# Where the empty rounds of a data-dependent block loop stand: after the full ones, or ahead of them

## The reference, cut to what matters

```python
h = silu(einsum('td,edf->tef', xf, w_gate)) * einsum('td,edf->tef', xf, w_up)
y = einsum('tef,te,efd->td', h, gate, w_down)
```

## Time and profile before

| | us |
|---|---|
| median of 3 runs (lowest, highest) | 1498.01 (1496.25, 1498.43) |
| the profiled execution's own time | 1493.46 |
| span of the profiled execution | 1491.6 |
| TensorE busy | 1439.3 (96%) |
| VectorE busy | 1015.0 (68%) |
| ScalarE busy | 770.8 (52%) |

### The profile page before, as it was taken

The page is one execution under the profiler, slowest core; times in us unless marked ns, Lnnn a source line. Parts: engine busy times, 40 slices in busy tenths (PEclk is TensorE's granted clock), DMA queues, the critical chain, the costliest instruction groups (busy, mean ns, idle before and its releaser), DMA issues.

```text
span 1491.6 us, 24267 instructions
## 1 busy us (share of the span) xinstructions
PE 1439.3 (96%) x9396; PEld 1291.7 (87%) x9396; DVE 1015.0 (68%) x1287; ACT 770.8 (52%) x912; POOL 190.4 (13%) x99
## 2 busy tenths in 40 slices
PE   8999999999999999999997999999999999999995
PEld 7999999999999999999996467888888888888772
DVE  4246746757777787523125668888888888888877
ACT  4245545444434433411110047777777777777774
POOL 0000000000000000234330001121121211222130
PEclk9999999999999999999998899999999999999998
DMA  7321231322213312633435699999999999999997
GB/s 262 123 89 57 86 114 61 96 90 86 88 57 115 116 58 73 205 111 146 145 96 205 207 394 375 384 401 391 392 375 384 384 382 398 387 390 401 348 294 232
DMA packets 74389, 335.36 MB, mean 225 GB/s; under 512 B 12086, under 2 KB 18790, under 8 KB 45514
## 3 DMA queue, kind: packets, MB, share of 16 engines
q1 hardware_dynamic: 68842, 315.54, 56.2%
q0 software_dynamic: 5472, 18.74, 5.0%
HBM read 313.56 MB, written 40.73 MB: 238 GB/s over the span
## 4 chain that ended last, share of the span: by engine, by line
PE 85%; DVE 7%; DMA 3%; ACT 2%; issue 2%; POOL 0%; ACTq 0%; SPq 0%; DVEq 0%; POOLq 0%
PE BANK L1811 13%; PE BANK L1812 13%; PE BANK L1813 13%; PE BANK L2170 7%; PE BANK L2172 7%; PE BANK L2171 7%; PE BANK L2222 4%; PE BANK L2220 4%; PE BANK L2221 4%; PE BANK L2154 2%; DMA RAWB<-in_w_up 2%; PE BANK L2183 2%; PE BANK L1953 1%; PE BANK L1829 1%; PE BANK L2050 1%
## 5 line engine op out<-in xcount | busy, mean ns | idle before, releaser
L1811 PE MATMUL BANK<-XH,HI 128*128 128x260 f32 x1746 | 503.0, 288 | 1.4 <-DVE RT L1487 1.0
L1683 DVE TENSOR_TENSOR LOB<-RAWB,HIB 128x2048 fp32r<-128x2048 f32 x196 | 448.6, 2291 | 74.0 <-ACT HIB L1050 73.1
L1812 PE MATMUL BANK<-XL,HI 128*128 128x260 f32 x1746 | 495.3, 284 | 0.0
L1813 PE MATMUL BANK<-XH,LO 128*128 128x260 f32 x1746 | 494.3, 283 | 0.0
L1050 ACT ACTIVATE HIB<-RAWB 128x2048 fp32r<-128x2048 f32 x196 | 376.4, 1921 | 86.0 <-PE BANK L2172 66.1
L1811 PEld LDWEIGHTS BANK<-XH,HI 128*128 128x128 f32 x1746 | 331.2, 190 | 2.7 <-issue 1.7
L1812 PEld LDWEIGHTS BANK<-XL,HI 128*128 128x128 f32 x1746 | 331.1, 190 | 0.7
L1813 PEld LDWEIGHTS BANK<-XH,LO 128*128 128x128 f32 x1746 | 330.9, 190 | 0.0
L2170 PE MATMUL BANK<-HIB,XGH 128*128 128x512 f32 x512 | 201.8, 394 | 5.5 <-issue 3.0
L2172 PE MATMUL BANK<-LOB,XGH 128*128 128x512 f32 x512 | 200.0, 391 | 0.0
L2171 PE MATMUL BANK<-HIB,XGL 128*128 128x512 f32 x512 | 199.8, 390 | 0.0
(11 more groups left out here) (388 smaller groups left out, 1674.5 us busy)
## 6 DMA issues: line engine op xcount, KB each, us to landing
RAWB<-in_w_down SPq DMA_DIRECT2D x68, 1024.0 KB, 9.5
RAWB<-in_w_gate SPq DMA_DIRECT2D x67, 1024.0 KB, 9.4
RAWB<-in_w_up SPq DMA_DIRECT2D x67, 1024.0 KB, 8.9
RAW<-in_w_in SPq DMA_DIRECT2D x39, 1024.0 KB, 4.9
RAW<-in_w_out SPq DMA_DIRECT2D x16, 1024.0 KB, 5.0
Y<-in_xT SPq DMA_DIRECT2D x8, 520.0 KB, 9.1
RT<-in_xT SPq DMA_DIRECT2D x16, 260.0 KB, 5.2
x_rows<-R SPq DMA_DIRECT2D x5, 832.0 KB
```

The costliest lines, as they stand in the source:

```text
L1683: dve.tensor_tensor(LOB[:, s, :], RAWB[:, r, :], HIB[:, s, :].bitcast(F32), ALU.subtract).then_inc(b_lo[s], 1)
L1811: pe.matmul(bank, hw[:, c, :], h, start=(c == 0), stop=False)
L1812: pe.matmul(bank, hw[:, c, :], l, start=False, stop=False)
L1813: ins = pe.matmul(bank, lw[:, c, :], h, start=False, stop=(c == KC - 1))
```

## The change: what it does

The loops keep their number of rounds, but the loop's own counter (now k) no longer names the block. `empty` is MAXB - last, that is 8 here (MAXB + 1 - (nb - 1), 9 here, on SyncE, whose rounds start at 2). A round has a body if `empty < k`. So rounds 1 to 8 (2 to 9 on SyncE) are empty, and the full ones follow. The number of the block stands in a register of its own, set ahead of the loop and raised by one at the end of each body. The body is the same otherwise; it is entered with j = 1, 2, and so on as before. The diff for TensorE and for SyncE (VectorE, ScalarE and GpSimd as TensorE):

```diff
-            with pe.Fori(1, MAXB) as j:
-                with pe.If(j < last):
+            empty = pe.snap(MAXB - last)
+            block_no = pe.alloc_register("block_pe")
+            pe.reg_mov(block_no, 1)
+            with pe.Fori(1, MAXB) as k:
+                with pe.If(empty < k):
+                    j = pe.snap(block_no, min_val=1, max_val=MAXB - 1)
                     gate_up(j, 0)
                     for n in range(4):
                         tokens(n, j + 1)
                         down(n, 8 + n, j)
                     turn_h(j, 4 * j + 7)
+                    pe.reg_add(block_no, block_no, 1)
             gate_up(last, 0)
```

```diff
-            with sp.Fori(2, MAXB) as j:
-                with sp.If(j < nb - 1):
+            empty = sp.snap(MAXB + 1 - (nb - 1))
+            block_no = sp.alloc_register("block_sp")
+            sp.reg_mov(block_no, 2)
+            with sp.Fori(2, MAXB) as k:
+                with sp.If(empty < k):
+                    j = sp.snap(block_no, min_val=2, max_val=MAXB - 1)
                     gate_up(j, 0)
                     down(j, 8)
+                    sp.reg_add(block_no, block_no, 1)
             gate_up(nb - 1, 0)
```

More of the change, by code:

```diff
@@ L780, in _ @@
             gather(1, p_rows, YO)
-            with pool.Fori(1, MAXB) as j:
-                with pool.If(j < last):
+            empty = pool.snap(MAXB - last)
+            block_no = pool.alloc_register("block_pool")
+            pool.reg_mov(block_no, 1)
+            with pool.Fori(1, MAXB) as k:
+                with pool.If(empty < k):
+                    j = pool.snap(block_no, min_val=1, max_val=MAXB - 1)
                     pool.wait_ge(b_tx, 4 * j + 4)
@@ L790, in _ @@
                     scatter(j)
+                    pool.reg_add(block_no, block_no, 1)
             pool.wait_ge(b_yw, 16 * last)
@@ L1094, in _ @@
                 bhi(i, 0, 1)
-            with act.Fori(1, MAXB) as j:
-                with act.If(j < last):
+            empty = act.snap(MAXB - last)
+            block_no = act.alloc_register("block_act")
+            act.reg_mov(block_no, 1)
+            with act.Fori(1, MAXB) as k:
+                with act.If(empty < k):
+                    j = act.snap(block_no, min_val=1, max_val=MAXB - 1)
                     for i in range(7, 10):
@@ L1119, in _ @@
                         bhi(i, 0, j + 1)
+                    act.reg_add(block_no, block_no, 1)
             for i in range(7, 10):
@@ L1711, in _ @@
                 token_lo(g, 1)
-            with dve.Fori(1, MAXB) as j:
-                with dve.If(j < last):
+            empty = dve.snap(MAXB - last)
+            block_no = dve.alloc_register("block_dve")
+            dve.reg_mov(block_no, 1)
+            with dve.Fori(1, MAXB) as k:
+                with dve.If(empty < k):
+                    j = dve.snap(block_no, min_val=1, max_val=MAXB - 1)
                     h_lo(j - 1)
@@ L1725, in _ @@
                     blo(1, 0, j + 1)
+                    dve.reg_add(block_no, block_no, 1)
             h_lo(last - 1)
```

## The result

The changed kernel takes 1506.32 us in the median of 20 runs, the kernel before 1497.52 us in 20 runs on the same chip. The ratio is 1.0058, with a 95% interval of 1.0047 to 1.0068: the change costs 8.7 us (7.0 to 10.2). The forecast was +3.8 us, 1501.8 us with a range to 1505.8. The direction was right; the size was less than half of what came, and the time lies outside the range.

The account below looks back on a forecast made before the run. TensorE, busy 96% of the span, was taken as the bound, so only its stalls could move. Entrance 6.2, code fetch 1.5 and clock 0.8, less 4.7 at the exit, gave +3.8 us: 1501.8 us, range 1498.8 to 1505.8.

Parts of the forecast that it names:

- TensorE's rounds at the entrance: Between `turn_h(0, 7)` and tile 0 of block 1: eight empty rounds stand wholly in the open, 6.0 us.
- register instructions: Ahead of the first body on TensorE: new instructions for `empty`, the block number and j cost 0.2 us.
- code fetch: TensorE's first empty round jumps over code not yet run and must wait for it: 1.5 us, between 0 and 4.5.
- tile 7 of block 1 (ScalarE): ScalarE's 4.6 us of rounds between tiles 6 and 7 replace a load's wait almost exactly: 0 us.
- clock behind the start: Behind the entrance, TensorE's half-clock stretch changes by -1.6 to +1.6 us; +0.8 taken.
- exit: Behind the loop: TensorE gains 3.2 us after `turn_h` and 1.5 us at the last block's tile 7, 4.7 us in all.
- (b): Entrance: TensorE's rounds are hidden, a gain of 4.7 us, 1493.3 us; chance 0.05 in full and 0.05 by half.
- (c): Entrance: SyncE's rounds delay block 2's first load past its use, 13.0 us late, 1514.8 us; chance 0.05.
- (d): TensorE's empty rounds: each fetches code anew, 14 us on top, 1516 us; chance 0.02.
- VectorE, GpSimd and SyncE at nothing: Entrance: the rounds of these three engines are covered by TensorE's delay or by later waits and cost 0.
- Rival (a): First jump at the entrance: no code has to be waited for, +2.3 us, 1500.3 us; chance 0.21.
- how long are they?: Length of TensorE's empty rounds at the entrance: 0.75 us each as in the kernel before, 6.0 us for eight.

Follow-up runs that it names:

- no_empty: Kernel before with each loop ending at the block count held in a register and no `If`, so no empty rounds on any engine: 1494.31 us, ratio 0.9978.
- first_hoisted: Changed kernel with `MAXB - last` put into a register ahead of the loop on all engines, so the `If` compares two registers: 1502.64 us, 1.0031 against before.
- last_costly: Kernel before, empty rounds still last, with the changed kernel's block register and an `If` that subtracts each round: 1501.46 us, ratio 1.0026.
- pe_first: Kernel before with only TensorE's empty rounds moved first, the other four engines keeping theirs behind: ratio 1.0041, +6.1 us.
- before_look2: Kernel before, unaltered, a single execution for a second profile; no timed difference.
- first_16: Changed kernel with 8 more rounds, so 16 empty ones first on each engine: 1517.61 us, ratio 1.0132 against before.
- others_first: Kernel before with only the empty rounds of VectorE, GpSimd and SyncE moved first, TensorE and ScalarE as before: ratio 0.9995, no difference.

## Why the prediction was wrong

By its own steps, what it gave and what the trace of the changed kernel has; "register instructions" and "clock behind the start" are what is left of the start's 8.43 us and of the entrance's 12.92 us:

```
                                   forecast   measured
TensorE's rounds at the entrance     6.0        7.8   (8 x 0.97)
register instructions                0.2        0.5   (8.43 - 7.8 - 0.16)
code fetch                           1.5        0.16
tile 7 of block 1 (ScalarE)          0          1.65
clock behind the start              +0.8       +1.25
clock behind tile 7's wait           -          1.6
exit                                -4.7       -4.74
sum                                  3.8        8.2
```

**Right:** that nothing hides TensorE's rounds at the entrance, since the sequencer arrives as the transposes start; the 0.68 us step became 9.11. That rivals (b), (c) and (d) would not come: the gap was far above 3 us, no load was late, and no empty round but the first had a long branch. The exit, both halves: 0.39 us from `turn_h` to tile 0 and no wait at tile 7, 4.74 us against 4.7, and -4.75 in no_empty, where it stands alone. VectorE, GpSimd and SyncE at nothing, in this kernel. Full rounds kept their 35.1 us. Rival (a), in which no code has to be waited for, had its condition nearly right (0.16 us) and its time wrong: 1500.3 us is 6.0 too low, by the two steps that follow.

**The step that failed: "how long are they?"** I took the round of before, 0.75 us, and the note that the body is unchanged. The condition was not: `j < last` compares two registers, `empty < k` an expression and a register, and the expression is evaluated where it is used. It costs a MOVE and an ALU_OP with their gaps, 0.21 us a round on TensorE and 0.16 to 0.18 on ScalarE. Taking it out (first_hoisted) gives back 8.7 - 4.6 = 4.1 us by the timed runs, whose intervals leave some 2.7 either way, and 3.55 on the ruler; putting it in at the other end (last_costly) costs 3.9 (2.1 to 5.8). That is most of the 4.9 that were missing. On TensorE it is 1.7 us at the start, where the small code fetch made up for it, so that the start as a whole, 7.7 forecast and 8.43 found, was nearly right by luck. So was the sum for first_hoisted, 3.8 against 4.6: the fetch of 1.5 us that was not paid stood in for the next term.

**The term that I had at nothing: ScalarE at the entrance.** I compared 4.6 us of rounds with the 5.04 us that a late load took, and called them equal, so that the 1.28 us of waiting at tile 7 would stay. In first_hoisted, where the rounds are as I counted them, the step from tile 6 to tile 7 is 5.59 us and the wait 1.82, 0.5 over before's; with the longer rounds they are 6.71 and 2.93. The 1.28 us themselves hung on the load and would have gone with TensorE's late start (pe_first has no wait there), so the whole 2.93 us and the clock behind them belong to ScalarE's rounds: 51.51 - 46.71 = 4.8 us on the ruler between pe_first and the changed kernel. And I had not asked what a longer wait there does to the clock: in before 1.28 us of idling left it at full, here 1.82 and 2.93 were both followed by 3.4 us at half, 1.6 us lost. A term of zero between two numbers 0.4 us apart had no upper end in my range. With 1.65 + 1.6 at that place, the range would have held the time. (Its upper end, 1505.8, is also 0.2 us more than the sum given for it, 1498.01 + 7.6.)

**The clock at the start.** +0.8 with bounds of ±1.6 held the 1.25 found. But I priced before's 3.3 us at half clock as 1.6 us that the change might save. They cost nothing there: before_look2 runs the same place at full clock and its entrance is 0.07 us shorter, as TensorE has to wait for tile 7's load either way.

**The code fetch** was mis-sized by 1.3 us in the other direction. The Trainium skill ("Runtime: NRT & Kernel Launch", Instruction fetch mechanics) has a taken branch to code outside the two current pages fetch it first. In this case the first jump of first_16 waited 5.0 us longer than a usual one, with a packet of q8 arriving meanwhile, which agrees; the first jump of the changed kernel waited 0.16 us. Between 910 and 1420 us, with fourteen of the loop's fifteen full rounds, the changed kernel's trace has no packet of q8. Before's exit had none either, and I set that against what the Trainium skill says; but no run shows over how many pages the body is spread, so it decides nothing. My upper bound of 4.5 us for the fetch was too low as well: first_16's 5.0 lies above it.

## What to carry to other kernels

A loop's empty round costs what the sequencer's instructions in it cost, and it is paid in full where the engine's queue is empty, that is, behind a wait; before moving such rounds, write down for each engine what it last waited for and how much work is queued. Count the condition as code: put a compared value into a register, or it is computed each round. Before adding up what an engine loses, look for what it waits for next: at before's entrance a load covered the first 2.4 us that TensorE lost ahead of it, and a start 8 us later used that up. Best is not to have the rounds: a loop whose end is in a register gained at the exit what the move was to gain, without the entrance (3.3 us by the timed runs).

## What the runs showed of the hardware

- A taken branch on TensorE's sequencer takes 214 to 224 ns (medians) and one not taken 83; on ScalarE both are 45 to 50 ns, on VectorE 56 to 63 in the median.
- The first jump over code that has not run took between 0.38 and 5.2 us; the nearest code packet ahead of the jump's end came from 16 us ahead of the loop's head to some 3 us behind it.
- The length of one gap of TensorE does not tell whether half clock follows, nor for how long. The 2.97 us at before's exit were not followed by it in one execution and were in the next; 2.40 us in others_first and 2.02 in before_look2 were not, 1.81 in pe_first and 1.82 in first_hoisted were, for 3.4 us. Behind 8.4 us of idling the half clock went on for 5.4 to 6.1 us of work, behind the 20.9 us of first_16 for 3.5. What decides it stays open.
- When TensorE was relieved of its rounds at the exit (pe_first), VectorE took over. Its 2.32 us of "issue" are in before's trace too, where TensorE's 2.97 cover them.
